# Seven products a pair instead of eight in the down projections of two feed-forwards

## The reference

```python
        h = rms_norm(x, ffn_norm_g[l])
        g = jnp.einsum('bld,df->blf', h, w_gate[l])
        u = jnp.einsum('bld,df->blf', h, w_up[l])
        x = x + jnp.einsum('blf,fd->bld', jax.nn.silu(g) * u, w_down[l])
...
        n2 = rms_norm_2(h, norm_mlp_pre[l])
        hid = jnp.square(jax.nn.relu(jnp.einsum('bsd,df->bsf', n2, w_up[l])))
        mlp_out = jnp.einsum('bsf,fd->bsd', hid, w_down[l])
        h = h + rms_norm_2(mlp_out, norm_mlp_post[l])
```

## Time and profile before

| | |
|---|---|
| median of 3 runs | 759.55 us (758.77 to 761.12) |
| the profiled execution | 758.59 us, its span 757.3 |
| TensorE busy | 739.8 us, 98% |
| VectorE busy | 457.8 us, 60% |
| ScalarE busy | 373.3 us, 49% |
| GpSimd busy | 112.5 us, 15% |
| moved by DMA | 130.46 MB, 172 GB/s |

### The profile page before, as it was taken

One profiled execution on the slowest core, in us unless ns is written; L12 is line 12 of the kernel. 1 busy time (PEld: TensorE's weight loads), 2 busy tenths in 40 slices (PEclk: granted clock), 3 DMA queues, 4 the chain that ended last, 5 costly groups with the idle time before them and its releaser, 6 DMA issues.

```text
span 757.3 us, 11043 instructions
## 1 busy us (share of the span) xinstructions
PE 739.8 (98%) x4394; PEld 641.1 (85%) x4394; DVE 457.8 (60%) x635; ACT 373.3 (49%) x535; POOL 112.5 (15%) x138
## 2 busy tenths in 40 slices
PE   6999999999999999999999999999999999999996
PEld 5877778999999999888888888888779899998895
DVE  5898695766555555465747555674948754455433
ACT  6666754644444434285443534664338644444431
POOL 2867550100000000001110000000302111001110
PEclk9999999999999999999999999999999999999999
DMA  9642142787665666446536543474535766656511
GB/s 318 207 132 82 58 160 92 229 284 220 189 212 172 195 216 208 133 142 219 169 110 195 194 139 112 123 250 147 178 107 198 260 192 187 206 184 191 180 46 56
DMA packets 70179, 130.46 MB, mean 172 GB/s; under 512 B 5312, under 2 KB 29072, under 8 KB 70128
## 3 DMA queue, kind: packets, MB, share of 16 engines
q1 hardware_dynamic: 68144, 125.00, 52.3%
q0 software_dynamic: 1552, 4.20, 1.7%
q10 hardware_dynamic: 432, 0.56, 0.2%
HBM read 128.62 MB, written 1.05 MB: 171 GB/s over the span
## 4 chain that ended last, share of the span: by engine, by line
PE 93%; DVE 3%; DMA 2%; issue 1%; ACT 1%; SPq 0%; DVEq 0%; ACTq 0%
PE psum L453 41%; PE psum L888 29%; PE psum L506 12%; PE psum L930 2%; DMA w_raw<-in_w_in 2%; PE psum L680 1%; PE psum L601 1%; PE psum L546 1%; PE psum L631 1%; PE psum L1058 1%; PE psum L582 1%; PE psum L652 1%; DVE b_ratio L2154 0%; PE psum L992 0%; PE psum L1020 0%
## 5 line engine op out<-in xcount | busy, mean ns | idle before, releaser
L1908 DVE TENSOR_TENSOR w_lo<-w_raw,w_hi 128x1024 fp32r<-128x1024 f32 x225 | 275.2, 1235 | 158.3 <-ACT w_hi L1284 157.7
L1284 ACT ACTIVATE w_hi<-w_raw 128x1024 fp32r<-128x1024 f32 x231 | 241.2, 1059 | 180.7 <-PE psum L888 78.6
L888 PE MATMUL psum<-h_hi,w_hi 128*128 128x256 f32 x608 | 170.3, 284 | 0.6 <-issue 0.6
L888 PE MATMUL psum<-h_hi,w_lo 128*128 128x256 f32 x608 | 169.5, 283 | 0.0
L888 PE MATMUL psum<-h_lo,w_hi 128*128 128x256 f32 x608 | 161.8, 281 | 0.0
L888 PEld LDWEIGHTS psum<-h_hi,w_hi 128*128 128x128 f32 x608 | 114.7, 189 | 1.7 <-issue 0.7
L888 PEld LDWEIGHTS psum<-h_hi,w_lo 128*128 128x128 f32 x608 | 114.4, 188 | 0.0
L888 PEld LDWEIGHTS psum<-h_lo,w_hi 128*128 128x128 f32 x608 | 111.1, 189 | 0.7
L453 PE MATMUL psum<-w_hi,h_hi 128*128 128x512 f32 (+1 forms) x240 | 94.5, 394 | 0.0
L453 PE MATMUL psum<-w_hi,h_lo 128*128 128x512 f32 (+1 forms) x240 | 93.0, 387 | 0.0
L453 PE MATMUL psum<-w_lo,h_hi 128*128 128x512 f32 (+1 forms) x240 | 92.9, 387 | 0.0
(11 more groups left out here) (303 smaller groups left out, 992.7 us busy)
## 6 DMA issues: line engine op xcount, KB each, us to landing
w_raw<-in_w_in SPq DMA_DIRECT2D x77, 512.0 KB, 4.5
w_raw<-in_w_down SPq DMA_DIRECT2D x54, 512.0 KB, 4.3
w_raw<-in_w_up SPq DMA_DIRECT2D x32, 512.0 KB, 4.4
w_raw<-in_w_gate SPq DMA_DIRECT2D x44, 256.0 KB, 2.9
w_raw<-in_w_up SPq DMA_DIRECT2D x44, 256.0 KB, 3.4
w_raw<-in_w_out SPq DMA_DIRECT2D x16, 512.0 KB, 4.0
w_raw<-in_w_branch_a SPq DMA_DIRECT2D x4, 512.0 KB, 4.6
w_raw<-in_w_branch_b SPq DMA_DIRECT2D x4, 512.0 KB, 4.6
```

The source lines that it names most:

```text
L888: mm = pe.matmul(outs, x[:, cols], y[:, kc, :], start=kc == 0 and n == 0, stop=kc == KC - 1 and n == (1 if i == 0 else 2))
L1284: act.activation(T.w_hi[:, k % SLOTS, :], T.w_raw[:, k % RAW_SLOTS, :], ACT.Copy).then_inc(S.w_rounded, 1)
L1908: dve.tensor_tensor(T.w_lo[:, k % SLOTS, :], T.w_raw[:, k % RAW_SLOTS, :], T.w_hi[:, k % SLOTS, :], ALU.subtract).then_inc(S.w_cut, 1)
```

## The change

The down product of a pair of 128-row blocks, with the two token tiles and the two halves of the output, is a 2 x 2 by 2 x 2 product of blocks. The change computes it with seven block products instead of eight (Winograd's form of Strassen's scheme), in all pairs but the last of each feed-forward. Each of the seven has a bank of its own over all pairs, and combinations on VectorE at the end make the four quarters of the output out of them. This is what it needs:

- **Weights of a pair** are loaded by GpSimd's queue, not SP's: three of the quarters of a 256 x 1024 block (`load_pair`, 768 KB) and the fourth twice (`load_twice`, 512 KB). The two sums of the fourth with the first two are made in the first feed-forward by a transfer that adds (`add_pair`, `accum_op=ALU.add`, 512 KB), in the second on VectorE. VectorE makes two more sums of 512 columns (`sum_pair`, `sum_pair_rest`). ScalarE and VectorE round and cut seven blocks of 128 x 512, in three parts.
- **Hidden rows** get four combinations on VectorE (`sum_hidden`, `_2`, `_3`), and seven blocks of 128 x 128 are rounded and cut.
- **Up products** are laid out by column tile: a fill is one column tile over all of K (`columns`), two of them go to the two halves of one bank (`up_two`), and ScalarE evacuates it (`take_up`, `take_hidden`). Only four slots of fills are used; the other four hold the parts of every second pair.
- **The ends** are rebuilt: the last pair is added as eight plain products to four of the banks (`down_quarters`) while VectorE combines the others. GpSimd no longer squares in the second feed-forward; ScalarE does. Constants are loaded between the pairs' transfers.

The core of the diff (`form` and `form_minus` are one addition or subtraction of a bank and a tile; QUARTERS, EARLY and the like are lists of products and banks):

```diff
+PRODUCT = {1: (1, 0, 2), 2: (3, 2, 0), 3: (7, 1, 1), 4: (2, 6, 6), 5: (5, 3, 5), 6: (6, 5, 3), 7: (4, 4, 4)}
+EARLY, LATE, MIXED, OWN = (1, 2, 3), (7, 5, 6, 4), (1, 6, 7, 5), (4, 2, 3)
...
+    def up_first(name, ready, rounded, spread, right=None):
+        k0 = W.first[name, 0]
+        for s, two in ((0, 0), (1, 0), (0, 1), (1, 1), (2, 0), (2, 1), (3, 0), (3, 1)):
+            ks = (k0 + 2 * two, k0 + 2 * two + 1)
+            if s == 0:
+                for k in ks:
+                    pe.wait_ge(*W.cut(S, k))
...
+    def down(q, products, first=False, last=False):
+        buf, i = pair_place(q)
+        pe.wait_ge(S.hidden_cut, q + 1)
+        for n_product, p in enumerate(products):
+            x, y, b = PRODUCT[p]
+            pe.wait_ge(S.pair_cut, pair_parts(q) + NEEDS[p])
...
+            for n, (u, v) in enumerate(((x_hi, y_hi), (x_hi, y_lo), (x_lo, y_hi))):
+                mm = pe.matmul(bank[b][:], u, v, start=first and n == 0, stop=last and n == 2)
...
+    down(LAST1 - 1, MIXED, last=True)
+    down(LAST1 - 1, OWN)
+    down_quarters(1, QUARTERS[1][:3])
+    turn_pairs(T.x, (0, 1), (5, 6), [[(S.x_added, 9)], [(S.x_added, 10)]])
+    down_quarters(1, QUARTERS[1][3:])
...
+    up_first("up2", CUT["h4"], NORM["h4"], False)
+    up_two(W.first["up2", 4], 3)
+    for i in range(2, PAIRS2):
+        if i > 2:
+            pe.wait_ge(S.up_taken, 2 * PAIRS1 + i)
+            up_two(W.first["up2", 2 * i], 7)
+        else:
+            pe.wait_ge(S.up_taken, 2 * PAIRS1 + 2)
+        down(FIRST2 + i - 2, EARLY, first=i == 2)
+        if i == 2:
+            pe.wait_ge(S.up_taken, 2 * PAIRS1 + 3)
+        down(FIRST2 + i - 2, LATE, first=i == 2)
```

ScalarE, the last rounds of the first feed-forward, and the rounds of the second:

```diff
+        round_hidden(i - 1)
+        round_pair(i - 1, 1)
+        round_pair(i - 1, 2)
+        if i == LAST1:
+            round_quarters(LAST1, 0)
+            round_quarters(LAST1, 1)
+        take_up(2 * i + 1)
...
+        if i < PAIRS2:
+            round_pair(q, 0)
+            round_hidden(q)
+            round_pair(q, 1)
+            if k < len(W.fills):
+                round_fill(k)
+            round_pair(q, 2)
+            take_hidden(i)
+            square_hidden(i)
```

VectorE, a round of the first feed-forward, the start and a round of the second, and the end of the first:

```diff
+        sum_hidden(i - 1, 2 * i)
+        cut_pair(i - 1, 0)
+        sum_hidden_2(i - 1)
+        scale_gate(2 * i)
+        sum_hidden_3(i - 1)
+        cut_fill(f + 4 * i + 4)
+        sum_pair(i - 1)
+        times_up(2 * i)
+        sum_pair_rest(i - 1)
+        cut_fill(f + 4 * i + 5)
+        cut_hidden(i - 1)
+        cut_pair(i - 1, 1)
+        cut_pair(i - 1, 2)
...
+    cut_fill(f + 4)
+    add_pair(FIRST2)
+    cut_pair(FIRST2, 0)
+    sum_pair(FIRST2)
+    cut_fill(f + 5)
+    sum_pair_rest(FIRST2)
+    cut_pair(FIRST2, 1)
+    cut_pair(FIRST2, 2)
+    sum_hidden(FIRST2, 2 * PAIRS1 + 1)
+    sum_hidden_2(FIRST2)
+    sum_hidden_3(FIRST2)
+    cut_fill(f + 6)
+    cut_hidden(FIRST2)
+    cut_fill(f + 7)
...
+            sum_hidden(q, 2 * PAIRS1 + i)
+            sum_hidden_2(q)
+            sum_hidden_3(q)
+            add_pair(q)
+            cut_pair(q, 0)
+            sum_pair(q)
+            cut_hidden(q)
+            sum_pair_rest(q)
+            cut_pair(q, 1)
...
+    p1, u, v21, v22, v12 = T.form[1]
+    dve.wait_ge(S.first_copied, 1)
+    form(1, 2, 3, p1, u, ALU.subtract)
+    step(add_x(p1, 1, 0))
+    own()
+    form_minus(1, 3, 4, u, v21)
+    form(1, 4, 5, u, v12)
+    own()
+    step(add_x(v21, 0, 0))
+    form(1, 4, 5, v21, v22, ALU.subtract)
+    step(add_x(v12, 1, 1))
+    own()
+    step(add_x(v22, 0, 1))
+    for n, (t, half, b) in enumerate(QUARTERS[1]):
+        dve.wait_ge(S.quarter_done, n + 1)
+        own()
+        add_x(bank[b][:], t, half).then_inc(S.x_added, 1)
```

GpSimd, the transfers of the first feed-forward:

```diff
+    def load_pair(q):
+        i = pair_place(q)[1]
...
+        elif q not in (0, FIRST2):
+            pool.wait_ge(S.pair_cut, pair_parts(q - 1))
+        pool.dma_start(T.pair_raw[i], W.pairs[q][:, 0:3, :]).then_inc(S.pair_landed[i], 16)
+    def add_pair(q):
+        i = pair_place(q)[1]
+        pool.wait_ge(S.twice_landed[i], pair_loads(q))
+        pool.dma_start(T.pair_t[:, i], W.pairs[q][:, 0:2, :], accum_op=ALU.add).then_inc(S.pair_added[i], 16)
+    for q in range(2):
+        load_twice(q)
+        load_pair(q)
+    for q in range(2, PAIRS1 + 1):
+        add_pair(q - 2)
+        if q < PAIRS1:
+            load_twice(q)
+            load_pair(q)
+        if q - 2 < CONST_DMAS:
+            load_const(q - 2)
```

More of the change, by code:

```diff
@@ L137, in __init__ @@
             self.slab((name, 0), a["w_out"][0][h * WIDE:(h + 1) * WIDE, :], 4, D)
[L138 to L149, removed]
+        for f in range(2 * PAIRS1):
+            self.first["up1", f] = len(self.fills)
+            for w in range(2):
+                self.fills.append([(lambda raw: raw, a["up1"][f, :, w, :])])
         win2 = a["w_in_2"][0]
@@ new lines, in down_quarters @@
+    def down_quarters(block, some):
+        q = (LAST1, LAST2)[block - 1]
+        buf, i = pair_place(q)
+        pe.wait_ge(S.hidden_cut, q + 1)
+        pe.wait_ge(S.pair_cut, pair_parts(q) + 2)
+        for t, half, b in some:
+            if b == 7:
+                pe.wait_ge(S.up_taken, 2 * PAIRS1 if block == 1 else 2 * PAIRS1 + PAIRS2)
+            for c in range(2):
+                y = ((0, 3), (2, 1))[c][half]
+                x_hi, x_lo = T.hid_hi[:, i, 2 * c + t, :], T.hid_lo[:, i, 2 * c + t, :]
+                y_hi, y_lo = T.pair_hi[buf][:, y, :], T.pair_lo[buf][:, y, :]
+                for n, (u, v) in enumerate(((x_hi, y_hi), (x_hi, y_lo), (x_lo, y_hi))):
+                    mm = pe.matmul(bank[b][:], u, v, start=b == 7 and c == 0 and n == 0, stop=c == 1 and n == 2)
+            mm.then_inc(S.quarter_done, 1)
@@ new lines, in scalar_program @@
+    f = W.first["up2", 0]
+    round_fill(f + 4)
+    round_pair(FIRST2, 0)
+    round_fill(f + 5)
+    round_pair(FIRST2, 1)
+    round_pair(FIRST2, 2)
+    take_hidden(0)
+    take_hidden(1)
+    square_hidden(0)
+    square_hidden(1)
+    round_fill(f + 6)
+    round_hidden(FIRST2)
+    round_fill(f + 7)
+    for i in range(2, PAIRS2 + 1):
+        q = FIRST2 + i - 1
+        k = f + 2 * i + 4
+        if i < PAIRS2:
[7 more added lines that the diff above has]
+            square_hidden(i)
+            if k < len(W.fills):
+                round_fill(k + 1)
+        else:
+            for part in range(2):
+                round_quarters(q, part)
+            round_hidden(q)
@@ L1886, in scalar_program @@
+    copy_first(2)
+    for n, (t, half, _) in enumerate(QUARTERS[2]):
+        square_last(n, t, half, T.last[t, half])
     act.wait_ge(S.x_posted, 8)
@@ L2407, in vector_program @@
[L2407 to L2415 removed]
+        gate = T.rows[:, j % 2, 0:SEQ]
+        dve.tensor_tensor(gate, gate, T.spread[:], ALU.mult).then_inc(S.gate_scaled, 1)
```

607 lines of the change are left out of this document (393 added, 214 removed).

## The result

The changed kernel takes 794.08 us (median of 4 runs, 790.61 to 796.78) against 759.55 us for the one before on the same chip (median of 3, 758.77 to 761.12): ratio 1.0448, 95% interval 1.0393 to 1.0504, 4.5% slower. A fourth run of the kernel before took 2571.8 us and is left out as disturbed. The forecast was 763.2, range 756 to 773. The profiled execution is the slowest of the four (796.78 us), and its span is 795.5 us, 38.2 more than before.

A forecast was written before the change was run, and what follows sets the result against it. TensorE was taken to bound both steady parts. Saved products, -17.5 us, and waits of 8.7, 5.0, 0.2, 0.2 and 3.6 gave +0.2; late adding transfers, 3.5, made +3.7 on the 759.55 median: 763.2, range 756 to 773.

The forecast's parts named there:

- The transfers that add: First feed-forward: adding transfers land a little late and TensorE waits, 3.5 us taken out of 0 to 14.
- case 4: Rival: adding transfers set the first feed-forward's round at 18.9 to 21.7 us, some less; 768 to 785 us, chance 0.14.
- The first pair: Start of the first feed-forward: pair 0 is cut by 159.9 and its sum must start by 168.5.
- The middle: Stretch between the two feed-forwards: predicted change 0.
- Start of the second feed-forward: TensorE waits 2.5 us for the fourth fill, then for the third evacuation, through VectorE's queue: cost 8.7 us.
- The case "faster": Rival: VectorE's queue at the second feed-forward's start is shorter, third evacuation at 594, transfers hidden; 755.5 us, chance 0.18.
- Steady part: Both feed-forwards stay bound by TensorE, at 16.41 and 10.62 us a pair, with 0 added by VectorE.
- The tie: Second feed-forward, steady part: VectorE needs 10.6 us a pair against TensorE's 10.62.
- case 5: Rival: VectorE sets the second feed-forward's round at 11.2 us a pair instead of 10.6; 768 us, chance 0.06.
- Ends: End of the first feed-forward: two waits of 2.5 us, cost 5.0; tail after the second: cost 3.6 us.
- The rule on additions in transfers: Adding transfers: an add reads two sources and runs at half a copy's rate; by it the fourth case comes true.

The follow-up runs named there:

- the early issue: The changed kernel with each adding transfer issued directly behind its own pair's loads, not behind the next pair's: 767.86 us, ratio 1.0120.
- the three moves: The early issue plus the first load of the second feed-forward later, `take_hidden` ahead of `round_pair(q, 2)`, and the last pair's cuts later: 756.06 us.
- the last kernel: The three moves plus the fourth fill rounded first, and VectorE's sums replacing adding transfers in the first feed-forward: 753.40 us, ratio 0.9923.

## Why the prediction was wrong, by its steps

**The transfers that add: the step that failed.** The price of a landing was right in the median: 12.9 us from the pair's cut, priced by the slope of the earlier trace rows, and 1.35 + 11.3 = 12.65 measured (11.3 to 15.1). When it is wanted was right too, 10.4 us after the cut. Wrong was the term made of it: 3.5 us out of 0 to 14, nearer the end at which the first slice's 318 GB/s would serve, with 4.3 us of ScalarE's order as a cover. The load behind which the adding transfer stands is issued when the pair before is cut, and that cut waits for the adding transfer before. This is a loop, and its lateness is paid in every round. The eight rounds from 165.37 to 316.90 us took 18.94 each where 16.41 was worked out: 1.0 to 4.8 late, 20.2 in sum. So even the upper end of 14 was short: the rounds beside 256 KB of constants were 2.5 and 3.1 late where some 1 was said, the second beside 512 KB 4.8 where 2.5 was said. And the bandwidth of the lower end was not there, with 270 to 307 GB/s while the engines were all but full. This was case 4, given 0.14, with rounds of 18.9 to 21.7 us and some less; measured 17.4 to 21.2. The time of 794.08 lies above its 768 to 785 as well, by about what the middle cost. Of the +23.6 us between the predicted and measured stage, the early issue gives back all, 28.8 at `z`.

**The first pair.** Its cut was put at 159.9 and came at 164.0. The adding transfer waited 5.2 us on GpSimd for its first load to land and took 11.1 itself; four loads were issued ahead of it. The sum had no row for this.

**The granted clock: left out.** Every term was a wait at full speed, and TensorE was put at some 720 us busy where 734.4 were measured. TensorE waited 26.0 us in the first feed-forward (18.7 for `up_rows`, 2.7 for fills, 1.3, 1.4 and 1.9 for the others), less the 7.0 saved is 19.0, and the stage grew by 25.3: the 6 us between are products at a lower clock, 0.84 in the window from 163.3 to 182.9 and 0.91 in the next. At the start of the second feed-forward it is 1.8 us for the 12 late products and 1.7 for the 72 ahead of them. The stalls cost 1.2 times their length in the first place and 1.4 in the second. The second of these varies from run to run: in the early issue's profile, with the same waits, the 72 products took 8.80 us and not 10.30.

**The middle: a term set to nothing.** GpSimd's first pair of the second feed-forward was thought to load in free time. It stood beside three fills of `w_out`, one of them on the path, in a stretch where the DMA engines were full, and cost 6 us. The prediction named no work that this load might delay.

**Start of the second feed-forward: right in place and cause.** The wait for the fourth fill was 2.4 (2.5 said), that for the evacuation 6.0, with `take_hidden` 29.0 us behind the start (27.6 said), and VectorE's durations as priced. The term was 8.7 and measured 12.1, the difference being the clock (1.8 + 1.7). The case "faster" needed VectorE 4 us earlier, and nothing of it came.

**Steady part: right.** Rounds of the second feed-forward are 10.53 us (638.46 to 775.34, 13 of them) where 10.62 was worked out, with VectorE busy 108.94 of 110 us. The tie holds, and case 5 fell; it is 1.2 us better than worked out over the 13 rounds. In the first, rounds are 16.28 once the transfers are early.

**Ends: right.** The wait at the last pair was put at 2.5 us and the one for `x` at 2.5. In the changed kernel they are 1.4 and 1.9; with the transfers early and the first load moved they are 2.7 and 1.9, 4.6 of the 5.0 said. From the last group's takeover to the end there are 20.2 us (20.1 worked out).

**The rule on additions in transfers.** The page "Collectives: The Full Stack" of the Trainium skill, section "The bandwidth ceiling: the fold count and why AG ≠ RS ≠ AR", states for ring collectives between cores that a reduction reads two sources and gets half the rate of a copy. The prediction took this over to a transfer that adds inside one core. The runs agree in sign: 11.3 us against 9.7 for the same 512 KB in the same place, and 270 to 307 GB/s against 331 to 355 over all that is under way then. That is 1.6 us from issue to landing and not a doubling; how much of either number is the wait behind the load ahead is not told apart, so the rate of the adding transfer alone is not shown. Case 4 came true, but not by this rule: its rounds are there with a landing that the slope of the earlier trace rows gives without a doubling.

**What stays open.** Of the 2.0 us by which the last kernel's middle is longer, 0.9 are the transposes and 0.7 the first 12 products of `z` (3.54 us, and 2.83 with the three moves alone); the rest was not followed. In the second feed-forward 9.4 of the 10.5 us saved are still lost, about 7 at its start and 3.7 in its tail. That the clock and not something else makes the 12 late products slow is read from the granted clock (0.50 for their first 3 us) beside their times; no kernel here took the wait away altogether. So it isn't shown what the start would be worth without it.

## What to carry to other kernels

Ask of each transfer what event lets it be issued, and whether that event waits for the same transfer one round earlier. If so, its latency and all that is queued ahead of it is part of the round, and its lateness counts once for each round, not once. Read the share of the DMA engines while the transfer is under way: over a whole round it was 0.67 to 0.77 here, and 0.87 to 1.01 where it mattered. Issue a transfer when its own inputs are there, not behind the next one's. When products are saved, price the stalls at the edges higher than their length, and look where the new loads meet a stretch that is short of bandwidth. Here 17.5 us of products came to 5.6 at the best (758.98 to 753.40).

## What was not expected of the hardware

- Behind some stalls TensorE is granted half its clock for a while. In the changed kernel, behind a wait of 6.0 us, the granted clock was 0.50 from 633.8 to 637.0, and the 12 products there took 4.59 us and not 2.80. A wait of 3.0 us left 4.36 in another kernel. In the first round of the first feed-forward 24 products of 256 columns took 3.1 us behind waits of 0.9 and 1.4 us, 4.5 to 4.6 behind 1.9 to 2.5, and 5.49 behind 3.0.
- Loads that meet from two queues share what the DMA engines can move: fills of 512 KB that land in 3.5 us (median) took 11.0 beside a constant of 512 KB and 1280 KB of GpSimd's queue, with the engines 0.94 busy at 299 GB/s, and 6.0 when the 1280 KB went later.
- A transfer that adds took 0.91 us of GpSimd to issue in the changed kernel and 0.53 as a plain copy, and it landed 1.6 us later than the copy by the medians. While it was under way the engines were as busy and moved 16% less on average.
